# Hybrid mixer: u and gate by blocks of 128 columns, another order of slabs, the attention's half of the output product in plain float32

## What is computed

```
def even_mixer(h, w_in, w_out, dw_w, dw_b, ln_g, ln_b):
    proj = h @ w_in                                   # 1024 -> 2560
    q, k, v, u, gate = jnp.split(proj, [512, 1024, 1536, 2048], axis=-1)
    a_out = merge_heads(stick_breaking_attention(split_heads(q, 8), split_heads(k, 8), split_heads(v, 8)))
    c = u * jax.nn.sigmoid(gate)                      # 512 channels
    c = causal_depthwise_conv(c, dw_w, dw_b)          # 31 taps
    c = jax.nn.silu(layer_norm(c, ln_g, ln_b))
    return jnp.concatenate([a_out, c], axis=-1) @ w_out
```

## Time and profile before

| | |
|---|---|
| median of 3 runs | 1667.57 us |
| the profiled execution | 1665.68 us, span 1663.9 us |
| TensorE (PE) busy | 1627.5 us, 98% |
| VectorE (DVE) busy | 1185.0 us, 71% |
| ScalarE (ACT) busy | 861.8 us, 52% |
| GpSimd (POOL) busy | 71.1 us, 4% |
| mean granted TensorE clock | 0.996 of 2.4 GHz |
| hybrid mixer's stage | from about 846 to 975 us |

### The profile page before, as it was taken

One profiled execution on the slowest core, in us unless ns is written; L12 is line 12 of the kernel. 1 busy time (PEld: TensorE's weight loads), 2 busy tenths in 40 slices (PEclk: granted clock), 3 DMA queues, 4 the chain that ended last, 5 costly groups with the idle time before them and its releaser, 6 DMA issues. The chain is left out here.

```text
span 1663.9 us, 24876 instructions
## 1 busy us (share of the span) xinstructions
PE 1627.5 (98%) x9431; PEld 1408.2 (85%) x9440; DVE 1185.0 (71%) x1778; ACT 861.8 (52%) x1212; POOL 71.1 (4%) x27
## 2 busy tenths in 40 slices
PE   8999999999999999999999999999999999999998
PEld 7987888888788887888889778888888889788887
DVE  2986788887578788666669876667666685766665
ACT  6334655573665556543566374435544465464443
POOL 5200000001600000000010000000000000000000
PEclk9999999999999999999999899999999999999999
DMA  8523466753335555555653235556555654436562
GB/s 284 187 102 112 163 200 203 215 168 129 105 129 186 193 178 184 190 188 190 218 173 128 80 128 185 188 190 202 167 200 181 223 178 142 134 132 198 181 200 78
DMA packets 211036, 283.35 MB, mean 170 GB/s; under 512 B 13196, under 2 KB 179075, under 8 KB 210963
## 3 DMA queue, kind: packets, MB, share of 16 engines
q1 hardware_dynamic: 209475, 278.18, 51.0%
q10 hardware_dynamic: 1488, 4.17, 0.7%
HBM read 280.88 MB, written 1.44 MB: 170 GB/s over the span
## 5 line engine op out<-in xcount | busy, mean ns | idle before, releaser
L579 ACT ACTIVATE w_hi<-raw 128x2048 fp32r<-128x2048 f32 x257 | 488.6, 1909 | 161.1 <-PE ps L2085 87.4
L1327 DVE TENSOR_TENSOR w_lo<-raw,w_hi 128x2048 fp32r<-128x2048 f32 x162 | 371.2, 2291 | 192.5 <-ACT w_hi L579 192.5
L2078 PE MATMUL ps<-x_pair,w_hi 128*128 128x512 f32 x1664 | 395.5, 390 | 0.0
L2078 PEld LDWEIGHTS ps<-x_pair,w_hi 128*128 128x128 f32 x1664 | 309.1, 188 | 62.0
L2085 PEld LDWEIGHTS ps<-x_pair,w_lo 128*128 128x128 f32 x1664 | 213.3, 191 | 8.1
L2085 PE MATMUL ps<-x_pair,w_lo 128*128 128x256 f32 x1664 | 215.9, 283 | 0.0
L1249 DVE TENSOR_TENSOR w_lo<-raw,w_hi 128x2048 fp32r<-128x2048 f32 x83 | 188.9, 2286 | 31.4 <-ACT w_hi L579 31.3
L1906 PE MATMUL ps<-x_pair,w_hi 128*128 128x256 f32 (+1 forms) x704 | 200.7, 285 | 2.4 <-DVE x_pair L1165 1.4
L1908 PE MATMUL ps<-x_pair,w_lo 128*128 128x256 f32 (+1 forms) x704 | 199.1, 283 | 0.0
L1907 PE MATMUL ps<-x_pair,w_hi 128*128 128x256 f32 (+1 forms) x704 | 199.1, 283 | 0.0
L1906 PE MATMUL ps<-w_hi,g_hi 128*128 128x512 f32 x480 | 187.5, 391 | 0.0
(11 more groups left out here) (189 smaller groups left out, 1749.0 us busy)
## 6 DMA issues: line engine op xcount, KB each, us to landing
raw<-in_ffn_w_in SPq DMA_DIRECT2D x80, 1024.0 KB, 5.1
raw<-in_ffn_w_out SPq DMA_DIRECT2D x44, 1024.0 KB, 4.9
raw<-in_ffn_w_up SPq DMA_DIRECT2D x40, 1024.0 KB, 5.1
raw<-in_ffn_w_down SPq DMA_DIRECT2D x22, 1024.0 KB, 5.3
raw<-in_hgrn_w_in SPq DMA_DIRECT2D x16, 1024.0 KB, 6.1
raw<-in_gla_w_in SPq DMA_DIRECT2D x12, 1024.0 KB, 5.2
raw<-in_hyb_w_in SPq DMA_DIRECT2D x10, 1024.0 KB, 5.8
raw<-in_ffn_w_in SPq DMA_DIRECT2D x16, 512.0 KB, 5.0
```

The source lines that it names most:

```text
L579: act.activation(w_hi[slot][:, :], raw[slot][:, :], ACT.Copy).then_inc(hi_done[slot], 1)
L1327: dve.tensor_tensor(w_lo[slot][:, :], raw[slot][:, :], w_hi[slot][:, :].bitcast(F32), ALU.subtract)\
L2078: pe.matmul(ps[:, bank, :], w_hi[s][:, at:at + P], x_pair[:, k, :, :].rearrange("p x t -> p (x t)"), start=k == 0, stop=False, skip_group_ ...
```

## The change

- `HYB_IN`: the order of slabs is u0, gate0, q0, k0, q1, k1, u1, gate1.
- u and gate go by blocks (`conv_block`): block c of u into the first half of one bank, block c of gate into that of another, and each block has its own sigmoid and its own multiplication. `begin` of both slots stands ahead of the pair.
- TensorE's order: logits of four heads, k1, u1 and gate1 (first block), rests of four heads, logits of four heads, the second block of u1 and gate1, values of four heads, rests and values of the other four. The attention's result goes into banks 6 and 7. The three `keep_warm` calls between them are gone.
- `convolve` takes the blocks that it may work on, and changes between them while more than one has taps left.
- The output product with slabs 0 and 1 is plain float32 (`project_plain`): from `raw` and an unsplit copy of the attention output. The slots are released for loading by SyncE, after TensorE has used them.
- GpSimd no longer does one of the low parts; VectorE does it.

```diff
-HYB_IN = ((2, 6), (3, 8), (2, 0), (3, 2), (0, 7), (1, 9), (2, 1), (3, 3))
+HYB_IN = ((2, 6), (3, 8), (2, 0), (3, 2), (0, 1), (1, 3), (2, 7), (3, 9))
+CONV_BANKS = ((4, 5), (2, 3), (6, 7), (4, 5))
...
+            def release_plain(s):
+
+                sp.wait_ge(slab_used[s], ring.uses[s] + 1)
+                sp.sem_inc(slab_ready[s], 1)
...
             load_out(hyb_out, HYB_OUT, HYB_OUT)
+            for s in HYB_OUT[:2]:
+                plain_full[s] = ring.dmas[s]
+                release_plain(s)
             load_ffn(3)
...
-            for s, n in ((0, 3), (1, 3), (2, 1), (3, 4)):
+            for s, n in ((0, 3), (1, 3), (2, 4), (3, 4)):
                 ring.skip(s, n)
-            low_one(2)
-            ring.skip(2, 2)
...
                     high_one(3)
-                    softplus_logs(0)
-                    softplus_logs(1)
-                    made[0] += 1
-                    sigmoid_gate(1, 1)
+                    evacuate(0, words(512, 512), bank=4)
+                    softplus_logs(0, 2)
+                    evacuate(1, words(1536, 512), 64 ** -0.5, bank=5)
+                    for s in HYB_OUT[:2]:
+                        ring.take(s)
                     stick_weights(0)
-                    high_one(0)
-                    high_one(1)
-                    evacuate(2, words(512, 512), bank=6)
                     stick_weights(1)
-                    high_one(2)
-                    evacuate(3, words(1536, 512), 64 ** -0.5, bank=7)
+                    made[2] += 1
+                    sigmoid_gate(2)
                     softplus_logs(2, 2)
+                    sigmoid_gate(3)
                     stick_weights(2)
                     stick_weights(3)
-                    high_one(3)
+                    high_one(2)
                     act.wait_ge(sb_pv, SB_HEADS)
                     for b in range(2):
-                        act.activation(x_hi[:, 2 * b:2 * b + 2, :], ps[:, 4 + b, :].rearrange("p (c t) -> p c t", t=SEQ), ACT.Copy)\
-                            .then_inc(x_hi_done, 1)
+                        act.activation(hyb["att"][:, 2 * b:2 * b + 2, :], ps[:, 6 + b, :].rearrange("p (c t) -> p c t", t=SEQ), ACT.Copy)\
+                            .then_inc(att_ready, 1)
+                    high_one(3)
...
-                    dve.memset(hyb["pad"][:, :, 0:pad], 0.0)
+                    link(dve.memset(hyb["pad"][:, :, 0:pad], 0.0))
...
+                    def convolve(n, *chunks):
+                        for i in range(n):
+                            left = [c for c in chunks if next_tap[c] < CONV_TAPS]
+                            c = next((c for c in left if c != latest[0]), left[0])
...
+                    gated(2)
+                    convolve(3, 2)
                     bounds(2)
+                    convolve(2, 2)
                     bounds(3)
-                    convolve(11)
+                    convolve(12, 2)
                     softplus(2)
                     softplus(3)
-                    convolve(16)
-                    low_of_banks(2)
-                    convolve(CONV_CHUNKS * CONV_TAPS)
+                    gated(3)
+                    convolve(20, 2, 3)
+                    low_one(2)
+                    convolve(8, 2, 3)
                     low_one(3)
+                    convolve(2 * CONV_TAPS - (3 + 2 + 12 + 20 + 8), 2, 3)
...
-                    slab_into(4, 2, x1)
-                    slab_into(5, 3)
+
+                    def conv_block(c, fresh=None):
+
+                        b = c % 2
+                        if b == 0:
+                            begin(2)
+                            begin(3)
+                        ins_u = features(2, CONV_BANKS[c][0], b * P, P, 0, fresh)
+                        if b:
+                            ins_u.then_inc(slab_used[2], 1)
+                        features(3, CONV_BANKS[c][1], b * P, P, 0).then_inc(slab_used[3] if b else block_pair, 1)
...
+                    def project_plain(slots, ks):
+
+                        for tb in range(NTB):
+                            for k in ks:
+                                s, kk = slots[k // 2], k % 2
+                                if tb == 0 and kk == 0:
+                                    pe.wait_ge(raw_full[s], plain_full[s])
+                                pe.wait_ge(att_ready, k // 2 + 1)
+                                for half in range(2):
+                                    at = kk * D + half * 512
+                                    ins = pe.matmul(ps[:, 2 * tb + half, :], hyb["att"][:, k, tb * P:tb * P + P], raw[s][:, at:at + 512],
+                                                    start=k == 0, stop=False, skip_group_check=True)
+                                if tb == NTB - 1 and kk == 1:
+                                    ins.then_inc(slab_used[s], 1)
...
                     heads(stick_logits, 0)
-                    slab_into(4, 0)
                     heads(stick_logits, 1)
                     slab_into(5, 1)
+                    conv_block(2)
                     heads(stick_rest, 0)
-                    slab_into(6, 2)
+                    heads(stick_rest, 1)
                     for s in range(2):
                         pe.wait_ge(proj_free[s], made[s] + 1)
-                    heads(stick_values, 0)
-                    heads(stick_rest, 1)
-                    slab_into(7, 3)
-                    all_copied()
                     heads(stick_logits, 2)
                     heads(stick_logits, 3)
+                    conv_block(3)
+                    pe.wait_ge(block_gated, 2)
+                    heads(stick_values, 0)
                     heads(stick_values, 1)
-                    keep_warm(18)
                     heads(stick_rest, 2)
                     heads(stick_rest, 3)
-                    keep_warm(4)
                     heads(stick_values, 2)
                     heads(stick_values, 3)
-                    keep_warm(8)
-
-                    base = x_new(6)
-                    project_out(HYB_OUT, lambda tb, k: base + k // 2 + 1, ks=range(4))
+
+                    base = x_new(4)
+                    project_plain(HYB_OUT, range(4))
                     conv_turned()
                     keep_warm(16, 4)
```

More of the change, by code:

```diff
@@ L1759, in _, with gated @@
-                    last_tap = {}
-                    taps = [(k, 2 * half + c) for half in range(2) for k in range(CONV_TAPS) for c in range(2)]
-                    def convolve(n):
-                        for _ in range(n):
-                            if not taps:
-                                return
-                            k, c = taps.pop(0)
+                    link(dve.memset(hyb["pad"][:, :, 0:pad], 0.0))
+                    def gated(c):
+                        u_slot, gate_slot = 2, 3
+                        if c % 2 == 0:
+                            dve.wait_ge(block_pair, c // 2 + 1)
+                            dve.wait_ge(block_gate, c // 2 + 1)
+                            done, count = block_gated, c // 2 + 1
+                        else:
+                            for s in (u_slot, gate_slot):
+                                used[s] += 1
+                                made[s] += 1
+                            dve.wait_ge(slab_used[u_slot], used[u_slot] + 1)
+                            dve.wait_ge(proj_free[gate_slot], made[gate_slot] + 1)
+                            done, count = proj_free[u_slot], made[u_slot] + 1
+                        dve.tensor_tensor(hyb["pad"][:, c, pad:pad + SEQ], ps[:, CONV_BANKS[c][0], 0:SEQ],
+                                          hyb["gate"][:, c // 2, c % 2, :], ALU.mult).then_inc(done, 1)
+                        dve.wait_ge(done, count)
@@ L1822, in _ @@
                     low_one(0)
+                    convolve(6, 0, 1)
                     low_one(1)
-                    convolve(16)
+                    convolve(4, 0, 1)
                     low_one(2)
+                    convolve(6, 0, 1)
+                    low_one(3)
+                    convolve(5, 0, 1)
+                    bounds(0)
+                    convolve(2, 0, 1)
+                    bounds(1)
+                    convolve(13, 0, 1)
+                    softplus(0)
+                    softplus(1)
@@ L2400, in _ @@
                     slab_into(7, 3)
-                    all_copied()
+                    copied = list(made)
+                    slab_into(4, 0)
+                    for s in range(1, RING):
+                        pe.wait_ge(proj_free[s], copied[s] + 1)
                     def stick_logits(hd):
@@ L2446, in heads @@
                         step(2 * pair + 1)
+                    def project_plain(slots, ks):
[11 more added lines that the diff above has]
+                                    ins.then_inc(slab_used[s], 1)
+                        for s in slots[ks.start // 2:ks.stop // 2]:
+                            used[s] += 1
@@ L2482, in _ @@
                     keep_warm(8, 4)
```

(4 more changed lines are left out.)

67 lines of the change are left out of this document (30 added, 37 removed).

## The result

| | before | after |
|---|---|---|
| median, 20 runs each, in turn on one chip | 1665.97 us (1662.35 to 1670.54) | 1670.94 us (1668.95 to 1675.25) |
| ratio | | 1.0034, 95% interval 1.0026 to 1.0043 |
| profiled execution | 1665.68 us, span 1663.9 | 1669.66 us, span 1667.9 |
| hybrid stage, transposes to next FFN (below) | 111.13 us | 114.48 us |
| VectorE taps in the stage (120) | 48.5 us, idle before them 0.0 | 52.6 us, idle before them 1.6 |

The change costs 5.0 us on the medians, 0.3%, which lies inside the 0.5% that this measurement can tell from no change, though the interval of the ratio does not hold 1. The forecast was 1669 with a range of 1661 to 1677.

The account below looks back on a forecast made before the run. TensorE was taken as the later stream, by only 3 us over VectorE's taps. Terms -0.2 (streams) and +2.8 (clock) sum to +2.6 us: 1668.3 from the profiled execution, 1670.2 from the median; forecast 1669, range 1661 to 1677.

Parts of the forecast that it names:

- The first block waits for both slabs: At the first block, u and gate are asked for together, so TensorE starts at 860.0: 3.8 us of new idle.
- TensorE up to the rests: TensorE's work from 860.0 through the first four rests takes 55.4 us, ending at 915.4.
- The gate of the third block: VectorE waits some 4.7 us for ScalarE's third-block sigmoid; this wait sets the rest.
- A tap on the same block: On VectorE, a tap following one on the same block takes 0.515 us, not 0.396; about 30 taps cost 3.6 us extra.
- rival 2: VectorE's dependent taps cost nothing extra, taking 3.6 us off the walk: 1665 us; chance 0.10.
- TensorE beside it: The plain float32 output product takes 13.8 us, 2.9 more on TensorE, hidden under VectorE's taps.
- Where the streams meet: At the turn of the convolved tokens, taps become the late stream: -0.2 us; TensorE idles 5.7 us before it.
- The clock: Half clock after TensorE's idle gaps at the first block and before the turn: +1.5 and +1.3, together 2.8 us.
- rival 3: TensorE's clock holds through both idle gaps, leaving -0.2 us: 1667 us, no change; chance 0.10.
- Rival 1: The clock falls inside attention's two runs of four logits heads, together +7.3 us: 1676 us; chance 0.25.
- Rival 4: At the turn, attention output comes last, not taps; end near 951, gain 4 to 6: 1661 us; chance 0.05.
- Queues: Next FFN's four loads begin at about 951 instead of 913.76, hidden, with about 8 us in hand for the first.

Follow-up runs that it names:

- e5: Changed kernel with the third block's sigmoid ahead of the exponentials of heads 0 to 3, VectorE's order kept: 1670.85 us.
- e9: Changed kernel with third- and fourth-block taps redirected to finished blocks so none reads the result before it (wrong convolution): 1666.06 us.
- e4: Changed kernel with ScalarE copying the attention output ahead of the third output slab's high part: 1670.69 us.
- e2: Changed kernel with 23 keep-warm products filling the gap ahead of the first block, the wait for gate's slab kept: 1667.93 us.
- e3: Changed kernel with 23 keep-warm products filling TensorE's idle time ahead of the turn of the convolved tokens: 1670.37 us.
- e10: Kernel before the change, with 4 keep-warm products in the 0.9 us wait ahead of the logits of heads 4 to 7: 1663.44 us.
- e0: The changed kernel measured once more without any edit: 1670.80 us, ratio to the kernel before 1.0020 to 1.0043.
- e1: Changed kernel with the wait for gate's slab moved behind u's 24 products in the first block: 1665.17 us.
- e6: Changed kernel with the third block's sigmoid early and 8, 4 and 5 taps around the bounds instead of 3, 2 and 12: 1666.85 us.
- e8: Changed kernel with blocks 2 and 3 adjacent, gate's slab awaited behind u, output copies and both sigmoids early: 1664.66 us.

## Why the prediction was right, and where not

- *The first block waits for both slabs*: right. 3.8 us of new idle were expected and 4.1 came; u was put at 860.0 and started at 860.42, on a clock that runs 0.2 later.
- *TensorE up to the rests*: right. With the 1.5 for the clock and the 0.2, 915.4 becomes 917.1; the four rests end at 917.19.
- *The gate of the third block*: the time is right (4.92 against 4.7), the sentence "this is the wait that sets the rest" is not. e5 took the wait away and the stage kept 114.30. The logits of heads 4 to 7 were just as late, so the wait was one of two of nearly the same length (4.9 and 4.2). That TensorE's stream sets both is what the walk should have said.
- *A tap on the same block*: 0.515 assumed, 0.521 measured, and e9 shows that the dependency is the cause. With it rival 2 falls. The Trainium skill (VectorE: DVE Perf Modes, The DRAIN you can't avoid) says that the next instruction does not start until the pipe is empty, with or without a semaphore after each, but also that one that is not held (need not wait for all earlier ones) starts earlier. Here independent taps follow in 0.396 while one lasts 0.48, and dependent ones in 0.521.
- *TensorE beside it*: right. The plain product takes 13.97 (13.8 expected), it is hidden (e4), and TensorE waits 5.3 before the turn (5.7 expected).
- *Where the streams meet*: right. The turn stands 1.16 later than before; less the 1.4 of the clock that is -0.2, as the sum had it.
- *The clock*: the mechanism right, the size of the second term too small for this profile. First gap 1.5 expected, 1.4 shown by e2 for this profile; the seven profiles that keep the gap put the first gate between 14.95 and 16.31 after the transposes, against 13.70 without the loss, so 1.25 to 2.6. Second gap 1.3 expected, 2.2 in this profile: 1.0 for the turn, as assumed, and 1.2 and not 0.3 for the keep-warm products behind it, which outlived the statistics. The six profiles with the whole gap need 9.63 to 11.05 from the turn to the next FFN, against 8.65 in e3, so it costs 1.0 to 2.4, and the 1.3 lay near its low end. Sum 2.6 expected, 3.35 in the profiles. The zero end, rival 3, is gone.
- *Rival 1, the clock falls inside the attention*: did not happen. Both runs of four heads kept the full clock in the changed kernel's profile; in the kernel before, it is most likely the fall that comes and goes. *Rival 4* needed the gate wait and the single-block taps to be wrong, and both came.
- *Queues*: right. The loads of the next FFN began at 951.74, and ScalarE waited for none.
- *From the sum to the time*: too low. The sum said +2.6 and the medians differ by 5.0. Of the 2.4 between them, 0.75 lie in the stage, where the keep-warm products behind the turn cost more than assumed. Another 0.65 lie in front of it and behind it, where nothing was changed. The last 1.0 is that the profiled execution of the changed kernel lies 1.3 below its median and that of the kernel before 0.3. That 1669 is within 2 us of 1670.94 is no merit of the sum: 2.4 us are little in 1670, the base of three runs (1667.57) was itself 1.6 above the median of twenty, and any sum from -5 to +11 would have ended in the range.
- *The base of the sum*: the weakest step. It was made against an execution with the fall (111.13) as if all were like it. Against the same stage at the full clock (107.60, e10) the change costs 6.9 us: 4.7 at the turn and 2.2 behind it. Where fewer executions of the kernel before lie above 1665 us than in the first comparison, the medians come near to that: they differ by 6.6 in e0, and by 6.9 in e4 and 7.6 in e5, whose edits left the stage almost as it was. With intervals 4 to 6 us wide this is a hint. That the fall is commoner in the first comparison is not shown, as only times are on record for it.

The 6.9 us can be put together from single edits: 4.4 at the first gap, wait and clock (e1), 2.1 for the clock at the second (e3), 3.5 in dependent taps (e9), less the 3.1 us that VectorE had in hand before (its last tap ends 3.1 ahead of the turn there, and 3.0 in e10). These are not shares that exclude others: e6 takes 2.5 off the same turn in another way. Nor is in them what the change saves, 30 keep-warm products and the splitting of two slabs. The products bridged waits. But on VectorE, which comes last now, two low parts stand between the gate of the third block and the last tap (940.48 and 945.85), where three stood behind the same gate before (two from 911.44 and one at 922.04), and the subtractions of the attention half (1.3 us) are gone. No run prices this by itself.

## What to carry to other kernels

Put a wait where its data is first read: one slab's wait moved 24 products down gave back 4.4 of 6.9 us, 1.4 of them the clock that fell after the idle time. When two streams are close, taking one wait away often uncovers another of the same length; ask what the engine does in the time that is freed, and move work there in the same edit. Before adding a sum to a median, see whether the profiled execution is one of the common kind.

## What was unexpected

The same idle gap costs a different amount each time: after 5.4 us without work the half clock lasted from TensorE's start for 3.2 us in the profile of the changed kernel and for 6.0 in e0 (from 862.40 to 868.4), with the same instructions. Behind gaps of 5.1 to 5.7 the turn took 1.97 in all six profiles that have one; behind 1.0, 1.8, 2.9 and, with four keep-warm products ahead, 2.05 it took 1.09. The Trainium skill (TensorE: Matmul & The Clock Gate, HAM oscillation) says that idle gaps put TensorE back to the half clock; the long ones did each time, and so did 3.34 us ahead of the rests in e8. Those of 2.9 and less ahead of the turn did not. In the profile of before the clock fell some 2 us behind a gap of 0.9, in the middle of small products; whether that gap brought it down is not shown.
